# Bringing the first tile's expert selection forward in a one-core hybrid decoder layer

## The reference

```
z  = rmsnorm(x) @ W_in                               # 1024 x 2432
ya = silu(layernorm(causal conv of width 31 (glu)))  # group A
yb = RWKV-7 time mixing                              # group B
yc = gate * conv3(...)                               # group C
yd = trailing means over 2, 4, 8, 16 positions       # group D
x  = x + concat(ya, yb, yc, yd) @ W_out
h  = rmsnorm(x);  q = h @ W_q                        # 8 heads, 2 halves of 128
s1, s2 = q against 128 keys each; top 16 of each; top 16 of the 256 sums
x  = x + sum over 8 heads x 16 experts of gate * gelu(u_e . h) * v_e
y  = rmsnorm(x)
```

## Time and profile before

| | |
|---|---|
| median of 3 runs (lowest, highest) | 1734.12 us (1733.38, 1738.78) |
| the profiled execution's own time | 1734.5 us |
| its span, first to last instruction | 1732.7 us |
| granted TensorE clock, mean | 0.843 of 2.4 GHz |
| busy, of the span: PE / DVE / ACT / POOL | 71% / 72% / 40% / 53% |
| expert rows, 520 gathers | 545.29 MB |
| other DMA | 55.90 MB |
| mean rate of all DMA | 348 GB/s |

### The profile page before, as it was taken

One profiled execution on the slowest core, in us unless ns is written; L12 is line 12 of the kernel. 1 busy time (PEld: TensorE's weight loads), 2 busy tenths in 40 slices (PEclk: granted clock), 3 DMA queues, 4 the chain that ended last, 5 costly groups with the idle time before them and its releaser, 6 DMA issues.

```text
span 1732.7 us, 19380 instructions
## 1 busy us (share of the span) xinstructions
PE 1232.9 (71%) x5360; PEld 619.5 (36%) x5360; DVE 1241.3 (72%) x2955; ACT 698.0 (40%) x1986; POOL 910.8 (53%) x1134
## 2 busy tenths in 40 slices
PE   5997898567777767767976767675766667666555
PEld 4886766322333333322322323232322222222110
DVE  3568755688887877768586778676767777767774
ACT  3321113455444444334345445343433343434444
POOL 0155120467576566555366656555656655656762
PEclk9999899778899898878986778778888887768878
DMA  6321147999999999999799999999999999999996
GB/s 173 122 98 49 37 137 100 318 390 418 414 415 416 407 418 419 417 417 398 255 388 417 419 417 416 417 378 418 419 417 418 418 418 412 409 417 402 420 415 255
DMA packets 110636, 602.42 MB, mean 348 GB/s; under 512 B 24752, under 2 KB 27184, under 8 KB 43968
## 3 DMA queue, kind: packets, MB, share of 16 engines
q0 software_dynamic: 74880, 545.29, 76.8%
q1 hardware_dynamic: 35648, 55.90, 11.0%
HBM read 597.96 MB, written 3.19 MB: 347 GB/s over the span
## 4 chain that ended last, share of the span: by engine, by line
DMA 39%; PE 27%; DVE 15%; POOL 6%; ACT 5%; issue 5%; DVEq 3%; POOLq 0%; SPq 0%; ACTq 0%
DMA arena<-in_uv,arena 38%; PE ps L985 10%; DVE arena L1848 8%; PE ps L553 5%; POOL arena L2072 4%; DVE arena L1320 3%; DVEq L1317 3%; PE ps L600 2%; POOL arena L2071 2%; PE ps L906 2%; PE ps L591 2%; DVE arena L1326 2%; PE ps L613 1%; PE ps L925 1%; ACT arena L1284 1%
## 5 line engine op out<-in xcount | busy, mean ns | idle before, releaser
L985 PE MATMUL ps<-arena 128*64 128x512 f32 x2048 | 662.8, 782 | 407.9 <-ACT arena L1284 407.7
L1848 DVE CUSTOM_DVE_ANT_0 arena<-arena 128x1024 f32<-128x1024 f32 x520 | 641.0, 1234 | 303.8 <-DMA arena<-in_uv,arena 285.0
L2072 POOL DMA_INDIRECT arena<-in_uv,arena x520 | 622.7, 1198 | 90.5 <-POOL arena L2071 8.7
L2071 POOL TENSOR_TENSOR arena<-arena 1x1 f32<-1x1 f32 x520 | 207.1, 398 | 534.9 <-PE ps L985 404.8
L985 PEld LDWEIGHTS ps<-arena 128*64 128x64 f32 x2048 | 152.1, 166 | 798.2 <-ACT arena L1284 553.2
L1278 ACT ACTIVATE arena<-arena 128x1 f32<-128x1 f32 x520 | 105.3, 202 | 757.3 <-DVE arena L1848 755.8
L1284 ACT ACTIVATE arena<-arena 128x64 f32<-128x64 f32 (+1 forms) x520 | 181.5, 349 | 17.0
L1280 ACT ACTIVATE arena<-arena 128x1 f32<-128x1 f32 x520 | 153.2, 295 | 16.9
L1320 DVE TENSOR_TENSOR arena<-arena 128x512 f32<-128x512 f32 (+7 forms) x310 | 132.6, 429 | 28.1 <-ACT arena L1032 18.9
L553 PE MATMUL ps<-arena 128*128 128x264 f32 (+1 forms) x608 | 141.9, 389 | 0.7 <-DVE arena L1320 0.7
L906 PEld LDWEIGHTS ps<-arena 128*128 128x128 f32 x1024 | 121.9, 198 | 34.9 <-issue 33.4
(11 more groups left out here) (161 smaller groups left out, 973.8 us busy)
## 6 DMA issues: line engine op xcount, KB each, us to landing
arena<-in_win SPq DMA_DIRECT2D x38, 512.0 KB, 3.3
arena<-in_wqk SPq DMA_DIRECT2D x64, 256.0 KB, 7.5
arena<-in_uv,arena POOLq DMA_INDIRECT x520, 12.3
arena<-in_wout SPq DMA_DIRECT2D x16, 512.0 KB, 7.8
arena<-in_xp SPq DMA_DIRECT2D x4, 512.0 KB, 7.5
arena<-in_wqk SPq DMA_DIRECT2D x16, 128.0 KB, 9.5
out_yp<-arena SPq DMA_DIRECT2D x4, 512.0 KB
arena<-in_const SPq DMA_DIRECT2D x1, 928.0 KB, 4.5
```

The source lines that it names most:

```text
L985: last = mm(ps[64 * q:64 * q + 64, b + c, :], diag[:, (s + q) % 8, :], ring[:, (s + q) % RING, D + 512 * c:D + 512 * c + 512], start=(s == ...
L1848: v.tensor_tensor_reduce(out=ring[:, s % RING, 0:D], in0=ring[:, s % RING, 0:D], in1=row, scale=1.0, scalar=0.0, op0=MUL, op1=ADD, accum_o ...
L2071: pool.tensor_tensor(carrier[:, 1:2], carrier[:, 0:1], carrier[:, 0:1], ALU.add).then_inc(S["carried"], 1)
L2072: pool.indirect_dma_start(out=ring[:, s % RING, :], out_offset=None, in_=a["uv"][:, :], in_offset=bass.IndirectOffsetOnAxis(ap=idx[:, t, s ...
```

## The change

- SyncE loads the 128 columns of the identity first, and the rest of the constants behind the first two weight blocks.
- TensorE runs four z columns in a row, and turns tiles 2 and 3 later; VectorE norms them later.
- The convolution's steps lie otherwise: 13 behind the bonus sum (8 before), none at level 4, three before and three after each chunk's update, so that the second group's steps stand in the chunk chain.
- The output product is made tile by tile: all eight blocks of tile 0, then four of tile 1, with two z columns between, then tile 0's second norm, query, score and selection. The other four blocks of tile 1 follow, three of them with weights in a buffer of their own (`w_aside`), and five z columns, the last behind tile 1's turns.
- Tile 1's selection (`choose(1, step)`) is made between the dots of unit 0.
- The state outputs of the convolution, the pool and the samples are issued before the output blocks. Query weights come in pieces between the weight blocks.
- GpSimd waits before gather 2 for tile 0's pair copies, not before gather 0 for those of both tiles.
- Mixer 1 starts at slot 8 and takes three ticks in four slots, not two in three. Its output products stand 3 to 4 ticks apart, not 1 to 2, and their eight weight blocks are released one by one with slots 152 to 166.
- The convolution's second group has its own scratch buffer and another PSUM bank.

```diff
-BLOCKS = [("z", j) for j in range(ZFRONT)] + [("out", j) for j in range(KT)] + [("z", j) for j in range(ZFRONT, len(ZORDER))]
+def out_blocks(t, lo, hi):
+    return [("out", KT * t + j) for j in range(lo, hi)]
+def z_blocks(lo, hi):
+    return [("z", j) for j in range(lo, hi)]
+BLOCKS = z_blocks(0, ZFRONT) + out_blocks(0, 0, 2) + z_blocks(ZFRONT, ZFRONT + 1) + out_blocks(0, 2, 6) + z_blocks(ZFRONT + 1, ZFRONT + 2) \
+    + out_blocks(0, 6, 8) + out_blocks(1, 0, 5) + z_blocks(ZFRONT + 2, len(ZORDER))
+ASIDE = (5, 6, 7)
...
-    return 2 * k // 3
+    return 3 * (k - START) // 4
...
-            sp_.dma_start(const, a["const"][:, :]).then_inc(d_const, 16)
+            sp_.dma_start(ident, a["const"][:, 0:128]).then_inc(d_ident, 16)
...
+            sp_.dma_start(const[:, 128:NCONST], a["const"][:, 128:NCONST]).then_inc(d_const, 16)
...
+                if n == n_out - 2:
+                    sp_.wait_ge(S["sample_copied"], 2)
+                    sp_.wait_ge(S["sample_in"], 3)
+                    sp_.dma_start(n2, a["n2"][0:1, :].partition_broadcast(128).rearrange("p a n -> p (a n)")).then_inc(d_n2, 16)
+                    sp_.wait_ge(S["samp_state"], 1)
+                    sp_.dma_start(a["o_swkv"][:, :, :, :], sst).then_inc(d_swkv, 16)
+                elif n == n_out - 1:
+                    sp_.wait_ge(S["conf_sum"], 1)
+                    sp_.dma_start(a["o_sconf"][:, :, :, :], extc[:, :, :, 1:CK]).then_inc(d_out, 16)
+                elif n == n_out:
+                    sp_.wait_ge(S["pool_in"], 1)
+                    sp_.dma_start(a["o_spool"][:, :, :, :], extp[:, :, :, 1:PB + 1]).then_inc(d_out, 16)
...
+                k = n - n_out - 8
+                if 0 <= k < 4:
+                    sp_.dma_start(wqk[:, 512 * k:512 * k + 512], a["wqk"][0][:, 512 * k:512 * k + 512]).then_inc(d_wqk, 16)
+                elif k == 4:
+                    sp_.dma_start(wqk[:, 2048:2304], a["wqk"][0][:, 2048:2304]).then_inc(d_k12, 16)
+                if n == n_out + 9:
+                    sp_.wait_ge(S["short_done"], 2)
+                    for i, j in enumerate(ASIDE):
+                        sp_.dma_start(w_aside[i], a["wout"][:, OUT_ORDER[j], :]).then_inc(d_aside, 16)
...
+                        sp_.wait_ge(S["slot_used"], W_SLOT + 2 * j)
...
+            def first_out(t, lo, hi):
+                for j in range(lo, hi):
+                    if t and j in ASIDE:
+                        pe.wait_ge(d_aside, 16 * len(ASIDE))
+                        w = w_aside[ASIDE.index(j)]
+                    else:
+                        n = BLOCK_OF[("out", KT * t + j)]
+                        pe.wait_ge(d_w[n % 3], 16 * (n // 3 + 1))
+                        w = wring[:, n % 3, :, :].rearrange("p a b -> p (a b)")
                     for nh in range(2):
-                        last = mm(ps[:, 2 * t + nh, :], ya[:, OUT_ORDER[j], 128 * t:128 * t + 128], w[:, 512 * nh:512 * nh + 512],
+                        last = mm(ps[:, (2, 5)[t] + nh, :], ya[:, OUT_ORDER[j], 128 * t:128 * t + 128], w[:, 512 * nh:512 * nh + 512],
                                   start=(j == 0), stop=(j == KT - 1))
-                if j < KT - 1 and tiles[-1] == 1:
-                    last.then_inc(S["block_used"], 1)
-                return last
+                    last.then_inc(S["block_used" if j < KT - 1 else "out_mm"], 1)
...
+                for k in range(3):
+                    yield C_OUT + 7 * k
                     project(k, 0)
-                    yield C_OUT + 3 * k + 1
+                    yield C_OUT + 7 * k + 4
                     project(k, 1)
...
+            pe.wait_ge(d_ident, 16)
             for t in (0, 1, TILES):
                 turn_x(t)
             pe.wait_ge(S["hT_done"], 3)
-            zcol()
-            turn_x(2)
-            zcol()
-            turn_x(3)
-            zcol()
+            zcol(4)
             first = Steps(mixer(0))
             for k in range(3):
                 first.until(E_LORA + 2 * k)
                 zcol()
...
-            first_out(0)
-            first_out(1)
-            first.until(C_LN + 3)
+            first_out(0, 0, 2)
+            zcol()
+            first.finish()
             pe.wait_ge(S["short_done"], 1)
-            first_out(2)
-            first_out(3)
+            pe.wait_ge(S["conf_out"], 1)
+            first_out(0, 2, 6)
+            zcol()
+            pe.wait_ge(S["rwkv_out"], 1)
+            first_out(0, 6, 8)
+            first_out(1, 0, 2)
             conf_mean(1)
-            pe.wait_ge(S["conf_out"], 1)
-            first_out(4)
-            first_out(5)
-            first.until(C_OUT + 3)
+            first_out(1, 2, 4)
             conf_variance(1)
-            zcol()
+            turned(0, 0)
+            turned(0, 1)
...
-            first.until(C_OUT + 9)
-            pe.wait_ge(S["conf_root"], 2)
             query(0)
-            first.finish()
-            zcol()
             score(0)
+            first_out(1, 4, 8)
+            zcol(len(ZORDER) - zn[0] - 1)
+            turned(1, 0)
+            turned(1, 1)
             zcol()
             query(1)
-            zcol()
             score(1)
-            zcol(len(ZORDER) - zn[0])
             def prepare(v, s):
...
-            act.wait_ge(S["xn2_done"], 2)
             queries(0)
-            zc()
+            conf_sigmoid(1)
+            act.wait_ge(d_const, 16)
             pair_copies(0, range(4))
             zc()
-            queries(1)
+            softmax(0)
+            zc()
+            second_squares(1)
+            root(1, "mean2", 2, "root2")
+            zc(len(ZORDER) - zn[0] - 1)
+            act.wait_ge(S["xn2_done"], 2)
             pair_copies(1, range(2))
             zc()
+            queries(1)
             pair_copies(1, (2, 3))
-            softmax(0)
-            zc(len(ZORDER) - zn[0])
-            softmax(1)
             later = Steps(mixer(1))
...
             first = Steps(mixer(0))
-            first.until(E_XS)
+            first.until(E_LORA + 6)
             norm(2)
             norm(3)
+            first.until(E_NORM + 3)
             features(2)
-            first.until(E_XS + 1)
+            first.until(E_BONUS)
             features(3)
-            first.until(E_LORA + 6)
-            first.until(E_BONUS)
             taps(4)
             first.until(E_BONUS + 2)
-            taps(8)
+            taps(13)
             for q in range(2):
                 first.until(C_G + 2 * q + 2)
-                taps(2)
+                taps(1)
             first.until(C_L1 + 3)
             for lv in range(1, LEVELS):
                 base = C_LV + 8 * (lv - 1)
                 for q in range(2):
                     first.until(base + 4 * q + 1)
-                    taps(1)
+                    taps(lv != 4)
                     first.until(base + 4 * q + 4)
-                    taps(1)
-                if lv == 3:
-                    taps(4)
+                    taps(lv != 4)
                 if lv == 4:
+                    assert made[0] == CK
                     conf_center(0)
+            first.until(C_P + 1)
             conf_scale(0)
-            taps(2)
+            first.until(C_P + 4)
             conf_swish(0)
-            first.until(C_P + 4)
-            taps(3)
             for c in range(GC):
                 first.until(C_CH + 6 * c + 1)
-                taps(2)
-                if c == 1:
+                if c == 2:
                     sample_output()
                 else:
-                    taps(2)
+                    taps(3)
                 first.until(C_CH + 6 * c + 3)
-                taps(2)
+                taps(3)
             first.until(C_LN + 2)
             taps(64)
-            first.until(C_LN + 9)
+            first.finish()
+            residual(0)
+            second_mean(0)
             conf_center(1)
-            first.finish()
+            second_norm(0)
+            second_features(0, 0)
+            second_features(0, 1)
...
+                    if u == 0:
+                        for step in range(3 * s // 2, 3 * s // 2 + (1, 2)[s % 2]):
+                            if step < STEPS:
+                                choose(1, step)
...
+            residual(1)
+            choose(0, STEPS - 1)
+            second_mean(1)
+            second_norm(1)
+            second_features(1, 0)
+            second_features(1, 1)
...
-            pool.wait_ge(S["xpair_done"], 2)
             for u in range(NU + 1):
                 t = UNITS[u][1] if u < NU else TILES
                 pool.wait_ge(S["idx_ready"], u + 1)
                 for s in range(TOPK if u < NU else SLOTS_S):
                     k = TOPK * u + s
                     later.until(pace(k - POOL_AHEAD))
-                    if k == 3:
+                    if k == 2:
+                        pool.wait_ge(S["xpair_done"], 1)
+                    elif k == 3:
                         pool.wait_ge(S["samp_out"], 1)
                     elif k == 4:
```

(3 more changed lines are left out.)

269 lines of the change are left out of this document (123 added, 146 removed).

## The result

The changed kernel takes 1715.1 us in the median (1711.0 to 1719.7, 4 runs; the kernel before 1735.7), a ratio of 0.988 (0.986 to 0.990). Run again on another chip it was 0.985 (0.9835 to 0.986). The forecast was 1681, with 1666 to 1706 as its range: the sign was right, the gain a little over a third of the 53 us I had summed. The profiled execution took 1719.7 us, the slowest of the four, 1717.8 of it span, so 14.8 less than the one that the sum was made against.

The account below looks back on a forecast made before the run. DMA engines full from about 320 us; before that, TensorE and VectorE delay the first gather. 13 + 11 + 2 + 14 + 1.2 - 3 + 17 - 2 = 53.2 off 1734.5 gave 1681 us, range 1666 to 1706.

Parts of the forecast that it names:

- Start: Up to the token turns: constants split, z columns back to back, fewer TensorE waits; 13 us gained, bounds 2 and 14.
- Taps: Convolution steps moved: 11 us gained (7 to 12) with level 4's wait gone, 2 us (0 to 4) after the levels.
- The shared port: Six VectorE steps beside GpSimd's short convolution: taken as stretched by half, 8.5 us; under full exclusion TensorE waits 3 to 5.
- Chunk chain to selection and gather: Chunk chain's end to tile 0's selection: 14 us gained (8 to 15); first gather without tile 1's pair copies: 1.2 us.
- Unit 0: First gathers, with tile 1's selection between the dots: 3 us lost, bounds 0 and 13.7.
- Output products: Second mixer's output products further apart, so gathers no longer stop: 17 us gained (5 to 22).
- Denser mixer: 3/4 instead of 2/3 tick a slot, 12% more second-mixer work per slot through unit 13: 2 us lost (0 to 6).
- VectorE takes it back: Rival: tile 1's selection costs its whole 13.7 us and products gain 5 instead of 17; 1704 us, chance 0.16.
- The clock: Rival: TensorE's granted clock falls to 1.2 GHz before 240 us; 1756 us at 120 us of such work, chance 0.03.

Follow-up runs that it names:

- run 10: Two edits on run 1's kernel: the rest of the constants loaded ahead of the tokens again, 1703.5 us; second group's output weight blocks loaded back to back again, 1700.4 us.
- run 1: Changed kernel with the short convolution's sample output (8-byte pieces) issued right behind the sample state's output, no longer ahead of the gathers: 1700.9 us, again 1700.7.
- run 5: The changed kernel measured again, unaltered, on another chip: 1712.1 us, 0.985 of the kernel before.
- run 3: Kernel before the change, with the sample output's DMA moved to behind the load of the second norm's weights: 1743.1 us, 1.0027.
- run 4: Tile 1's selection, all steps but the last, done ahead of unit 0's first dot: 1706.3 us on the changed kernel, 1705.8 on run 1's kernel.
- run 8: Run 1's kernel with query product 2 behind unit 0's third pair of slots: 1700.1 us; also with the last z column ahead of tile 1's turns: 1703.0.
- Run 9: On run 1's kernel: second mixer slower up to slot 98, 1701.3 us; 64 extra VectorE copies in units 1 to 4, 1713.5, or in units 18 to 21, 1706.0.

## Why the prediction was wrong, point by point

- *Start, 13 us.* 10.0 in this profile, 11.2 in the changed kernel's second one, and 9.8 to 13.2 over all 17 profiles with this start. The waits went as listed. The first term, 2.1 us for the constants, is the doubtful one: moved back, they cost the token turns 0.6 us, which is inside the spread (run 10).
- *Taps, 11 and 2.* 11.0 and 1.4: level 5 starts at 160.57 instead of 181.56, the chunk chain at 182.27 instead of 204.66, and TensorE's wait of 10.46 us is gone. The z columns also covered the six steps a chunk: the chain to the head sums takes 31.6 us, 31.4 before.
- *The shared port.* VectorE and GpSimd behind the last chunk:

```profile
209.84 2.80 DVE L1349 SCALAR_TENSOR_TENSOR arena<-arena 128x256 f32<-128x256 f32 x6
...
213.48 6.92 DVE L1349 SCALAR_TENSOR_TENSOR arena<-arena 128x256 f32<-128x256 f32 x6
```

```profile
212.31 9.23 POOL L1928 TENSOR_TENSOR arena<-arena 128x512 f32<-128x512 f32 x7 [43.04 <-ACT arena L1047]
```

  Six convolution instructions beside GpSimd's short convolution took 6.92 us here, 2.80 alone, a stretch of 2.5 where I had taken 1.5. TensorE waited 0.20 us behind them. The Trainium skill, SBUF — State Buffer, Who interferes with whom, says that of two such instructions the second to issue waits until the first has finished. In the prediction I read that as a wait behind all seven of GpSimd's, but the rule goes instruction by instruction. By it the six of VectorE and some five of GpSimd in these 6.92 us would have taken 2.80 + 5 x 1.27 = 9.2 us, an estimate (one GpSimd instruction of this size took 1.27 us at 134.89, the seven here 1.32 each). So the trace bears out contention, which VectorE pays, and not a full exclusion.
- *Chunk chain to selection and gather, 14 and 1.2.* 6.2 (7.9 in the changed kernel's second profile), less than even the low end of 8 and 1.2. This step failed, and at the place that I had named for that end: TensorE waited 0.94 and 4.71 us for output weights, and the eight matmuls behind the second wait took 6.28 us instead of 3.60, at a granted clock of 0.66 in that window. Together 8.3 of the 9 missing in this profile. I had worked out 6 MB in the same 12 us, 14.6 us of DMA time, and then left it to the bound. A transfer that needs longer than its window belongs in the sum.
- *Unit 0, 3 us lost.* 16.9. The main failure. The prediction had the 8-byte pieces in view and put them at nothing (they "keep the DMA engines busy meanwhile"). I had asked what VectorE does between the dots and had not followed what SyncE does at the moment the gathers start. Of the steps that move I counted the instructions, but not that query product 2 waits for head 1's weights, whose issue stands in SyncE's order behind o_ssc, and that all of it now meets the gathers earlier. Moving one DMA gives 11 to 14 us back (runs 1, 5), and up to 340 us the loss is then 12.4 us, 2.1 more than in the kernel before. That 2.1 lies near the 3 in part by luck, since the kernel before pays for the pieces there too: without them its gathers lose only 3.9 us in their first 36 us (run 3), by which estimate unit 0 itself costs some 8. What these 8 us are stays open; the selection's place between the dots isn't it (run 4), nor the wait for query weights alone (run 8).
- *Output products, 17.* 13.6, and 12.9 in the second profile: the right size. That it comes from the products' distance is not shown; only the spreading of the loads is ruled out (run 10). One stretch of 296 GB/s stays.
- *Denser mixer, 2 us lost.* Counted to 760 us, 9.3. I took it as a share of VectorE's work, while VectorE was no busier than before. Run 9 shows that more work on VectorE costs time there, but a slower pace brought nothing clear of the spread, so what takes the 9.3 us stays open.
- *Rivals.* "VectorE takes it back" had the time that came nearest, 1704, but its terms aren't what happened: doing the selection first is no faster once the weights are in time (run 4), and the products gained 13.6, not 5. The clock was no bound: granted 0.98 up to the first gather, and 0.95 in the kernel before.
- *A slip in the sums.* 545 MB at 419 GB/s take 1,301 us, 2.50 a gather, not 1,304 and 2.51. Nothing rests on it.

The forecast's own test had "I am wrong if TensorE waits for weights in the product part". It did. It also had every stretch around the products above 350 GB/s and the gathers at full rate from about 280 us, and neither came. What I had not written down as a test is the one that cost most: a transfer issued late by a queue that seemed idle.

## What to carry to other kernels

When a start is pulled forward, list every queue that shares that moment, in order, and for each entry who waits for it; a DMA in tiny pieces belongs where nobody behind it in the same queue is awaited, and that place has to be looked for anew in each version (the same move won 11 to 14 us here and lost 5 in the kernel before). A reorder that looks right or wrong should be tried again after the largest stall is gone: the selection's place looked 6 to 9 us better ahead of the dots before that, and 5 us worse after, each hardly clear of the noise.

## What was not expected of the hardware

- Issues on SyncE's queue take 0.43 us, or 1.97 us right behind the pieces in the kernel before; but 27.18, 21.60, 24.23 and 21.66 us behind them with gathers in flight. The pieces themselves landed 13.1 and 15.2 us after their issue where no gathers ran (runs 3, 1), and 42.6 and 38.5 with gathers. The Trainium skill, DMA: Bandwidth & Descriptors, Queues, rings and completion order, says that a DMA engine takes turns between its queues packet by packet. By that rule a small packet can wait for a large one of the gathers each time, and that the pieces land later beside gathers agrees with it; nothing finer was looked at. Why SyncE itself is held until then is not shown.
- 2,048 pieces of 8 bytes keep the DMA engines at a share of 1.10 and more at 69 to 88 GB/s in the kernel before (303 to 313 us). With the pieces elsewhere its gathers lose 6.4 us less in their first 36 us (run 3), so 16 KB cost some 6 to 8 us of all engines.
- The same early part differs by up to 5 us between executions: the second head sums came at 222.14 and 219.67 in two profiles of one kernel, of which the first had a granted clock of 0.66 at 180 to 190 us and the second 1.00, and at 217.68 to 222.53 over all profiles with this early part.
